# The first ten blocks of a mixer's input projection multiplied as whole fp32, without their split into two parts

## The chip, the cores and the metric

The kernel runs on one core of a Trainium2 chip. The metric is the device time of one execution in microseconds (us), the median of several runs. The engines are named PE (TensorE, matmuls), PEld (its weight loads), DVE (VectorE), ACT (ScalarE), POOL (GpSimd) and SP (SyncE, which here issues the loads from memory). Each runs its own list of instructions in order and waits on semaphores.

## What is computed

Two transformer blocks over 256 tokens of width 1024, all in fp32. The change sits in the first layer of the second block, in its mixer:

```python
h = x @ w_in
q, f_pre, i_v, g, a, a_gate = jnp.split(h, [...], axis=-1)   # six times 512 columns
f = lb + (1.0 - lb) * jax.nn.sigmoid(f_pre)                  # gated linear attention: f, k, q, v
k = (1.0 - lb) * jax.nn.sigmoid(-f_pre)
# heads: chunkwise scan over q, k, v, log f, then a norm and a gate with g
# convolution: u = a * sigmoid(a_gate), 31 taps over time per channel, layer norm, silu
# y = concat(heads, convolution) @ w_out
```

In front of it stands the end of the first block: `h + sigmoid(norm(h) @ w_ple_gate + b) * norm(p @ w_ple_proj)`, whose result is the mixer's x.

## The kernel before

All weights come as a stream of blocks of 128 x 1024 fp32 (512 KB), 8 tiles of 128 x 128 each. The list `LAYOUT` (L76) gives their order; around the change it is `ple_gate` (8 blocks), `ab_in` (20), `ab_g` (4), `mem1b` (4), `ab_out` (8). The ring of raw buffers `w_raw` has `RAW` = 4 places, the rings `w_hi` and `w_lo` of the parts `RING` = 4.

To get fp32 accuracy from the faster fp32r matmuls, each block is split: ACT writes `w_hi`, the rounded copy (`part_hi`, L499 to L506), and DVE writes the remainder `w_lo` = `w_raw` - `w_hi` (`part_lo`, L1012 to L1016). x is split likewise into `x_hi` and `x_lo`. `three` (L1803) issues three matmuls per tile: hi with hi, hi with lo, lo with hi (L1805 to L1807). `chunk` (L1813) does a block of 8 tiles this way with 256 moving columns and then counts up `block_done`.

Order is written out by hand. Each engine calls `blk()` once per block; on ACT and DVE that issues the parts of the block four further on (`behind`). So block b's parts are made while TensorE is at block b - 4. `w_hi` of block b waits for its load and for the end of block b - 4; SP loads block b when `lo_ready` says that the remainder of block b - 4 is made, since the raw buffer is free from then on (L472).

The 20 blocks of `ab_in` are, by n in the loops at L875 (ACT), L1646 (DVE) and L2338 (PE): n = 0 to 7 the pairs of convolution value and gate for the four channel groups, 8 to 11 f, 12 to 15 q, 16 to 19 the values. For odd n under 8, ACT takes the sigmoid of the gate (L879) and DVE forms the product into `ub` (L1652). The convolution runs on DVE: `conv_taps` (L1608) issues the next taps, 31 for each of 4 channel groups, 124 in all, each a multiply-add over 128 x 256 (L1620; the first of a group is L1617). `beside` (L1645) says how many stand behind each n, `comes` (L1605) from which total on a group may begin; of the two lowest open groups it alternates. A tap waits for the tap before it of its own group. Six more stand at L1672, up to eight around each head's state scan (L1688, L1691), and the rest behind (L1701).

x of the mixer is written by DVE (`embed`, L1579): the gate block c of `ple_gate` is scaled (L1589), ACT takes its sigmoid (L867), DVE multiplies (L1582) and adds into `xs` (L1583, `res_ready`). Then ACT makes `x_hi` (L871) and DVE `x_lo` (L1597), and TensorE's first two `ab_in` blocks go tile by tile together (`two_chunks`, L1822).

Behind the heads, ACT's list has the remaining `mem1b` blocks (L936), then `x_hi` of the heads (L947), then the norm of the convolution (L949). TensorE's output projection (L2437) starts when DVE has made `x_lo` of the heads (L1738).

Of the kernel before, what the change touches and what calls it, by code (L numbers as in the profile page):

```python
# [16 lines left out]
P = 128  # L17
# [25 lines left out]
TILES = 8  # L43
# [39 lines left out]
for _name, _count in LAYOUT:  # L83
    FIRST[_name] = NB
    NB += _count

# [58 lines left out]
def build(nc, x_d, mem_d, pT, prm_d, id_d, cst_d, late_d, w_d, out):  # L145
    with ExitStack() as ctx:
# [307 lines left out]
        def _(sp):  # L454
# [8 lines left out]
            for b in range(RAW, NB):  # L463
# [8 lines left out]
                sp.wait_ge(lo_ready, b - RAW + 1)  # L472
# [22 lines left out]
        def _(act):  # L495
# [3 lines left out]
            def part_hi(b):  # L499

                act.wait_ge(raw_in[b % RAW], 16 * (b // RAW + 1))
                if b >= RING:
                    act.wait_ge(block_done, b - RING + 1)
                if FIRST["pool"] <= b < FIRST["pool"] + 2:
                    act.wait_ge(pool_w, b - FIRST["pool"] + 1)
                nc.scalar.activation(w_hi[:, b % RING, :], w_raw[:, b % RAW, :], ACT.Copy).then_inc(hi_ready, 1)  # L506

            def behind(b):

                if b + RING < NB:  # L510
                    part_hi(b + RING)
# [424 lines left out]
            mem_blocks(1, 4, 6)  # L936
# [57 lines left out]
        def _(dve):  # L994
# [17 lines left out]
            def part_lo(b):  # L1012

                dve.wait_ge(hi_ready, b + 1)
                nc.vector.tensor_tensor(w_lo[:, b % RING, :], w_raw[:, b % RAW, :], w_hi[:, b % RING, :].bitcast(F32),  # L1015
                                        ALU.subtract).then_inc(lo_ready, 1)  # L1016

            def behind(b):

                if b + RING < NB:  # L1020
# [578 lines left out]
            embedded_lo(0, 2)  # L1599
            embed(DC - 1)  # L1600
            embedded_lo(2, DC)
# [3 lines left out]
            taps, made, comes = [0] * CC, [0] * CC, (0, 9, 20, 31)  # L1605
# [39 lines left out]
            beside = {1: 9, 3: 11, 5: 11, 7: 5, 8: 6, 9: 6, 10: 5, 11: 5, 12: 4, 13: 1, 14: 4, 15: 2, 16: 0, 17: 2, 18: 4, 19: 4}  # L1645
# [25 lines left out]

            conv_taps(6)  # L1672
# [120 lines left out]
        def _(pe):  # L1793
# [6 lines left out]
            def arrived(b):  # L1800
                pe.wait_ge(lo_ready, b + 1)
# [7 lines left out]
            def tile(b, n, w=P):  # L1809
                s = slice(n * P, n * P + w)  # L1810
                return w_hi[:, b % RING, s], w_lo[:, b % RING, s]
# [63 lines left out]
            def token_turns(blocks, outs, chunks, hi, lo, start, stop, first=None, ready=None, between=None, ahead=0):  # L1875

                for t in range(2):
                    s = slice(t * P, (t + 1) * P)
                    for i, b in enumerate(blocks):
                        if t == 0 and i >= ahead:  # L1880
                            arrived(b)
                        for k, c in enumerate(chunks[i]):
# [3 lines left out]
                            w = (ahead_hi[i][:, o], ahead_lo[i][:, o]) if i < ahead else (w_hi[:, b % RING, o], w_lo[:, b % RING, o])  # L1886
# [22 lines left out]
            def token_rows(b, outs, chunks, w, hi, lo, start, stop=False, ready=None):  # L1909

                arrived(b)
                for k, c in enumerate(chunks):
                    if ready:
                        ready(c)
                    for t in range(2):
                        s, o = slice(t * P, (t + 1) * P), slice(k * w, (k + 1) * w)
                        ins = three(outs[t][:, 0:w], hi[:, c, s], lo[:, c, s], w_hi[:, b % RING, o], w_lo[:, b % RING, o],
# [3 lines left out]
            def token_last(b, outs, chunks, hi, lo):  # L1921

                arrived(b)
                for t in range(2):
                    s = slice(t * P, (t + 1) * P)
                    for k, c in enumerate(chunks):
                        o = slice(k * HALF, (k + 1) * HALF)
                        ins = three(outs[t][:, :], hi[:, c, s], lo[:, c, s], w_hi[:, b % RING, o], w_lo[:, b % RING, o],
# [710 lines left out]
```

## Time and profile before

| | us |
|---|---|
| median of 3 runs | 1341.74 (1340.62 to 1345.08) |
| the profiled execution, its own time | 1341.19 |
| its span, first to last instruction | 1339.2 |
| PE busy | 1283.6 (96%) |
| DVE busy | 869.7 (65%) |
| ACT busy | 664.6 (50%) |

The rows below are of the profiled execution, with times counted from the start of its span. In a timeline a row can stand for several instructions of the same kind in a row (xN); its time is then from the start of the first to the end of the last. In brackets stand the idle time ahead of it and what ended it. Neighbouring matmuls overlap, so a matmul's cost in a queue is the distance between two starts and not its duration. The mixer's stage lies between about 592 and 752 us.

### The profile page before, as it was taken

Reading aid. Unit: us, or ns where it says so; the run is one execution under the profiler, and the core shown is the slowest. Engines: PE = TensorE matmul, PEld = TensorE weight load, DVE = VectorE, ACT = ScalarE, POOL = GpSimd, SP = SyncE. Lnnn points to the kernel's source line nnn. Section 1 sums busy time; section 2 is a strip of 40 time slices with the busy share of each in tenths; the row PEclk is TensorE's granted clock in tenths of the full one; section 3 lists DMA queues with packets and bytes.
Section 4 is the critical chain, followed back from the end, with each engine's and each line's share of the span. In section 5 each row is a group of like instructions: output and inputs, shape, how many; then the busy total and the mean of one; then the engine's idle time right before and its main releaser. Section 6 shows DMA issues by size and latency. Waiting matters only on the chain.

```text
span 1339.2 us, 18113 instructions
## 1 busy us (share of the span) xinstructions
PE 1283.6 (96%) x7204; PEld 1115.2 (83%) x7204; DVE 869.7 (65%) x1443; ACT 664.6 (50%) x995; POOL 5.3 (0%) x7
## 2 busy tenths in 40 slices
PE   8999999999999999999888899999999999999997
PEld 7888888997788888899877787788888987788886
DVE  5665567878676555679997665545557664654555
ACT  5654446657464444555614544544444554544443
POOL 0000000000000000000000000000001000000000
PEclk9999999999999999999978999999999999999999
DMA  7555555532455555454422432555554532455551
GB/s 280 175 188 190 187 186 187 189 115 80 147 176 185 188 188 186 149 174 158 158 79 95 143 126 95 205 175 186 189 179 151 174 127 95 157 174 181 189 185 58
DMA packets 61571, 215.84 MB, mean 161 GB/s; under 512 B 6576, under 2 KB 9904, under 8 KB 61232
## 3 DMA queue, kind: packets, MB, share of 16 engines
q1 hardware_dynamic: 61056, 213.15, 46.2%
q10 hardware_dynamic: 432, 1.54, 0.3%
q8 instruction: 57, 0.93, 0.3%
q14 instruction: 26, 0.21, 0.0%
HBM read 213.62 MB, written 1.05 MB: 160 GB/s over the span
## 4 chain that ended last, share of the span: by engine, by line
PE 80%; DVE 13%; ACT 4%; issue 1%; DMA 1%; SPq 0%; ACTq 0%; DVEq 0%
PE bank L1805 24%; PE bank L1807 24%; PE bank L1806 24%; DVE w_lo L1015 3%; DVE arena L1620 3%; PE bank L1985 1%; PE bank L1872 1%; ACT w_hi L506 1%; PE bank L2083 1%; PE bank L2123 1%; ACT xs L645 1%; DMA w_raw<-weights_d 1%; PE bank L2094 1%; DVE xs L1691 0%; DVE rt L1065 0%
## 5 line engine op out<-in xcount | busy, mean ns | idle before, releaser
L1015 DVE TENSOR_TENSOR w_lo<-w_raw,w_hi 128x1024 fp32r<-128x1024 f32 x395 | 481.9, 1225 | 368.4 <-ACT w_hi L506 367.2
L506 ACT ACTIVATE w_hi<-w_raw 128x1024 fp32r<-128x1024 f32 x395 | 416.7, 1059 | 537.7 <-PE bank L1807 525.6
L1805 PE MATMUL bank<-w_hi,x_hi 128*128 128x512 f32 (+2 forms) x992 | 372.7, 376 | 13.2 <-DVE x_lo L1033 6.6
L1807 PE MATMUL bank<-w_hi,x_lo 128*128 128x512 f32 (+2 forms) x992 | 367.2, 370 | 0.0
L1806 PE MATMUL bank<-w_lo,x_hi 128*128 128x512 f32 (+2 forms) x992 | 367.0, 370 | 0.0
L1805 PEld LDWEIGHTS bank<-w_hi,x_hi 128*128 128x128 f32 x992 | 187.1, 189 | 48.9 <-issue 10.9
L1807 PEld LDWEIGHTS bank<-w_hi,x_lo 128*128 128x128 f32 x992 | 186.9, 188 | 31.8
L1806 PEld LDWEIGHTS bank<-w_lo,x_hi 128*128 128x128 f32 x992 | 187.2, 189 | 30.2
L1805 PE MATMUL bank<-w_hi,h_hi 128*128 128x512 f32 (+1 forms) x364 | 142.3, 391 | 0.0
L1807 PE MATMUL bank<-w_hi,h_lo 128*128 128x512 f32 (+1 forms) x364 | 141.3, 388 | 0.0
L1806 PE MATMUL bank<-w_lo,h_hi 128*128 128x512 f32 (+1 forms) x364 | 141.2, 388 | 0.0
L1805 PE MATMUL bank<-x_hi,w_hi 128*128 128x256 f32 x352 | 102.7, 292 | 8.1 <-DVE x_lo L1033 2.9
L1806 PE MATMUL bank<-x_lo,w_hi 128*128 128x256 f32 x352 | 100.2, 285 | 0.0
L1807 PE MATMUL bank<-x_hi,w_lo 128*128 128x256 f32 x352 | 100.1, 284 | 0.0
L1805 PEld LDWEIGHTS bank<-w_hi,h_hi 128*128 128x128 f32 x364 | 68.4, 188 | 14.7 <-DVE h_lo L1033 1.2
L1807 PEld LDWEIGHTS bank<-w_hi,h_lo 128*128 128x128 f32 x364 | 68.3, 188 | 14.1
L1806 PEld LDWEIGHTS bank<-w_lo,h_hi 128*128 128x128 f32 x364 | 68.4, 188 | 13.4
L1805 PEld LDWEIGHTS bank<-x_hi,w_hi 128*128 128x128 f32 x352 | 68.1, 193 | 10.1 <-DVE w_lo L1015 3.8
L1806 PEld LDWEIGHTS bank<-x_lo,w_hi 128*128 128x128 f32 x352 | 68.1, 194 | 0.2
L1807 PEld LDWEIGHTS bank<-x_hi,w_lo 128*128 128x128 f32 x352 | 68.1, 193 | 0.0
L1620 DVE SCALAR_TENSOR_TENSOR arena<-arena,prm 128x256 f32<-128x256 f32 x120 | 50.8, 478 | 0.6
L1805 PE MATMUL bank<-m_hi,w_hi 128*128 128x256 f32 x128 | 38.7, 302 | 0.0
(307 smaller groups left out, 1390.4 us busy)
## 6 DMA issues: line engine op xcount, KB each, us to landing
w_raw<-weights_d SPq DMA_DIRECT2D x395, 512.0 KB, 3.2
arena<-weights_d SPq DMA_DIRECT2D x4, 512.0 KB, 6.2
arena<-late_d SPq DMA_DIRECT2D x1, 1056.0 KB, 5.7
xs<-x_d SPq DMA_DIRECT2D x2, 512.0 KB, 5.9
kv_mem<-mem_d ACTq DMA_DIRECT2D x1, 1024.0 KB, 7.2
out_d<-xs SPq DMA_DIRECT2D x4, 256.0 KB, 2.8
cst<-cst_d SPq DMA_DIRECT2D x1, 671.0 KB, 10.2
arena<-pT_d ACTq DMA_DIRECT2D x1, 256.0 KB, 2.7
```

What stands on the lines that cost most here:

```text
L506: nc.scalar.activation(w_hi[:, b % RING, :], w_raw[:, b % RAW, :], ACT.Copy).then_inc(hi_ready, 1)
L645: nc.scalar.activation(xs[:, c, 0, s], turned_n(v, c, t), ACT.Identity, scale=col("ln_g", LN_COL[v] + c), bias=col("ln_b", LN_COL[v] + c)) ...
L1015: nc.vector.tensor_tensor(w_lo[:, b % RING, :], w_raw[:, b % RAW, :], w_hi[:, b % RING, :].bitcast(F32), ALU.subtract).then_inc(lo_ready, 1)
L1620: ins = nc.vector.scalar_tensor_tensor(conv[:, c, :], src, w, conv[:, c, :], ALU.mult, ALU.add)
L1805: nc.tensor.matmul(out, wh, xh, start=start, stop=False, skip_group_check=True)
L1806: nc.tensor.matmul(out, wh, xl, start=False, stop=False, skip_group_check=True)
L1807: return nc.tensor.matmul(out, wl, xh, start=False, stop=stop, skip_group_check=True)
L1872: nc.tensor.matmul(PB[banks[t]][:, c % 4 * P:c % 4 * P + P], xs[:, c, 0, t * P:(t + 1) * P], res_i, start=False, stop=False, skip_group_ch ...
L1985: ins = nc.tensor.transpose(PB[2 + k][:, at:at + P], hf[:, t, (2 * k + j) * P:(2 * k + j + 1) * P], ident)
L2083: ins = nc.tensor.matmul(half(n % 2, t), xq[:, 2 * h + k, t * P:(t + 1) * P], k_mem[l][:, 2 * h + k, :], start=k == 0, stop=k == 1)
L2094: ins = nc.tensor.transpose(PB[2 + n % 2][:, k * S + t * P:k * S + (t + 1) * P], e_buf(n)[:, 0, t, k * P:(k + 1) * P], ident)
L2123: ins = nc.tensor.matmul(o[:, c * S:(c + 1) * S], v_mem[l][:, k, at:at + P], pt_buf(n)[:, k, :], start=k == 0, stop=k == 1)
```

## The change

The blocks n = 0 to 9 of `ab_in` (`WHOLE`) are no longer split. TensorE multiplies `w_raw` by `xs` in one fp32 matmul per tile (`whole_chunk`), as soon as the block's load has landed and the chunk of x is written. ACT and DVE leave out their parts. The parts are counted and placed by `parts_of` and `slot`, which leave the whole blocks out, instead of by the block's number. The raw buffer of a whole block is free when `block_done` says that TensorE has finished it, so SP waits for that. `two_chunks` is no longer used for `ab_in`; each block goes by itself.

The taps are dealt out anew: `beside` has 90 instead of 79 taps in the loop, `comes` is (0, 12, 26, 40), and the six taps behind the loop are gone (they stand in the rest at the end). On ACT one `mem1b` block is moved behind `x_hi` of the heads. On DVE the last `embed` comes ahead of all `x_lo`.

```diff
+WHOLE = range(FIRST["ab_in"], FIRST["ab_in"] + 10)
+def parts_of(b):
+    return b + 1 - min(max(b + 1 - WHOLE.start, 0), len(WHOLE))
+def slot(b):
+    return (parts_of(b) - 1) % RING
+def slot_before(b):
+    c = b - 1
+    while c >= 0 and (c in WHOLE or parts_of(c) != parts_of(b) - RING):
+        c -= 1
+    return c
...
-                sp.wait_ge(lo_ready, b - RAW + 1)
+                if b - RAW in WHOLE:
+                    sp.wait_ge(block_done, b - RAW + 1)
+                else:
+                    sp.wait_ge(lo_ready, parts_of(b - RAW))
                 sp.dma_start(w_raw[:, b % RAW, :], w_d[b]).then_inc(raw_in[b % RAW], 16)
...
-                if b >= RING:
-                    act.wait_ge(block_done, b - RING + 1)
+                if slot_before(b) >= 0:
+                    act.wait_ge(block_done, slot_before(b) + 1)
...
-                if b + RING < NB:
+                if b + RING < NB and b + RING not in WHOLE:
                     part_hi(b + RING)
...
-            mem_blocks(1, 4, 6)
+            mem_blocks(1, 4, 5)
...
             for h in range(HG_HEADS):
                 act.wait_ge(hy_f, h + 1)
                 nc.scalar.activation(x_hi[:, h, :], ho[:, h, :], ACT.Copy).then_inc(hy_hi, 1)
+            mem_blocks(1, 5, 6)
...
-                if b + RING < NB:
+                if b + RING < NB and b + RING not in WHOLE:
                     part_lo(b + RING)
...
-            embedded_lo(0, 2)
             embed(DC - 1)
-            embedded_lo(2, DC)
+            embedded_lo(0, DC)
...
-            taps, made, comes = [0] * CC, [0] * CC, (0, 9, 20, 31)
+            taps, made, comes = [0] * CC, [0] * CC, (0, 12, 26, 40)
...
-            beside = {1: 9, 3: 11, 5: 11, 7: 5, 8: 6, 9: 6, 10: 5, 11: 5, 12: 4, 13: 1, 14: 4, 15: 2, 16: 0, 17: 2, 18: 4, 19: 4}
+            beside = {1: 12, 3: 14, 5: 14, 7: 8, 8: 5, 9: 5, 10: 5, 11: 5, 12: 4, 13: 1, 14: 4, 15: 2, 16: 0, 17: 3, 18: 4, 19: 4}
...
-            conv_taps(6)
-
...
+            def whole_chunk(b, out, x, ready):
+
+                pe.wait_ge(raw_in[b % RAW], 16 * (b // RAW + 1))
+                for k in range(TILES):
+                    ready(k)
+                    ins = nc.tensor.matmul(out, w_raw[:, b % RAW, k * P:(k + 1) * P], x[:, k, 0, :], start=k == 0, stop=k == TILES - 1)
+                ins.then_inc(block_done, 1)
...
-                if n == 0:
-                    two_chunks(b, (half(4, 0), half(5, 0)), x_hi, x_lo, operand(4))
-                elif 1 < n < 16:
-                    chunk(b, half(4 + n % 4, 0), x_hi, x_lo)
+                elif n < 2:
+                    pe.wait_ge(gate_z, 7 + n)
+                if b in WHOLE:
+                    whole_chunk(b, half(4 + n % 4, 0), xs, lambda k: pe.wait_ge(res_ready, k + 1))
+                elif n < 16:
+                    chunk(b, half(4 + n % 4, 0), x_hi, x_lo, operand(4))
```

## Rows read from the trace of the kernel before

**Rows 1.** The page, busy us and share of the span of each engine.
```profile
PE 1283.6 (96%) x7204; PEld 1115.2 (83%) x7204; DVE 869.7 (65%) x1443; ACT 664.6 (50%) x995; POOL 5.3 (0%) x7
```

**Rows 2.** The chain of waits from 560 to 760, its shares by line.
```profile
by line: DVE arena L1620 20.7%; DVE w_lo L1015 15.5%; PE bank L1805 11.3%; PE bank L1806 10.7%; PE bank L1807 10.7%; issue 3.4%; DVE xs L1691 3.2%; ACT w_hi L506 2.6%; PE bank L1872 1.8%; PE bank L2404 1.4%; PE bank L1865 1.3%; DVE arena L1
```

**Rows 3.** Busy time by stretch (length; PE, PEld, DVE, ACT, POOL; clock; DMA).
```profile
599.50:670.50 71.00, 63.96 (x532) 62.51 (x531) 67.94 (x120) 41.62 (x60) 0.00 (x0) 1.00 0.44 149
670.50:706.00 35.50, 27.15 (x209) 26.00 (x209) 32.57 (x78) 6.62 (x14) 0.00 (x0) 0.77 0.22 75
```

**Rows 4.** TensorE's timeline, 591 to 722 (start, us, instruction, idle before and releaser).
```profile
591.90 0.28 PE L1806 MATMUL bank<-x_lo,w_hi 128*128 128x256 f32 x1
592.02 0.28 PE L1807 MATMUL bank<-x_hi,w_lo 128*128 128x256 f32 x1
595.19 0.36 PE L1805 MATMUL bank<-x_hi,w_hi 128*128 128x256 f32 x1 [2.89 <-DVE x_lo L1033]
...
619.06 0.39 PE L1805 MATMUL bank<-x_hi,w_hi 128*128 128x256 f32 x1 [0.61 <-DVE arena L1652]
...
626.02 0.39 PE L1805 MATMUL bank<-x_hi,w_hi 128*128 128x256 f32 x1 [0.95 <-DVE arena L1652]
...
674.21 1.01 PE L2400 MATMUL bank<-arena 128*128 128x128 f32 x3 [6.81 <-DVE xs L1691]
...
705.99 0.69 PE L2416 MATMUL bank<-ident,arena 128*128 128x128 f32 x2 [3.40 <-DVE arena L1620]
...
721.33 0.47 PE L1805 MATMUL bank<-w_hi,x_hi 128*128 128x512 f32 x1 [1.90 <-DVE x_lo L1033]
```

**Rows 5.** TensorE's timeline near 792: whole fp32 matmuls, two records each.
```profile
792.23 1.89 PE L2123 MATMUL bank<-arena,kv_mem 128*128 128x256 f32 x8
793.96 1.89 PE L2083 MATMUL bank<-kv_mem,arena 128*128 128x256 f32 x8
```

**Rows 6.** DVE's timeline, 593 to 706.
```profile
593.12 0.42 DVE L1583 TENSOR_TENSOR xs<-bank,arena 128x256 f32<-128x256 f32 x1
...
602.07 2.36 DVE L1015 TENSOR_TENSOR w_lo<-w_raw,w_hi 128x1024 fp32r<-128x1024 f32 x2 [2.50 <-ACT w_hi L506]
...
605.26 4.13 DVE L1620 SCALAR_TENSOR_TENSOR arena<-arena,prm 128x256 f32<-128x256 f32 x8
...
618.92 4.43 DVE L1620 SCALAR_TENSOR_TENSOR arena<-arena,prm 128x256 f32<-128x256 f32 x11
...
625.55 0.42 DVE L1652 TENSOR_TENSOR arena<-bank,arena 128x256 f32<-128x256 f32 x1
...
634.88 1.21 DVE L1015 TENSOR_TENSOR w_lo<-w_raw,w_hi 128x1024 fp32r<-128x1024 f32 x1
...
670.43 1.22 DVE L1015 TENSOR_TENSOR w_lo<-w_raw,w_hi 128x1024 fp32r<-128x1024 f32 x1
...
685.09 1.23 DVE L1015 TENSOR_TENSOR w_lo<-w_raw,w_hi 128x1024 fp32r<-128x1024 f32 x1 [1.32 <-ACT w_hi L506]
...
700.49 5.43 DVE L1620 SCALAR_TENSOR_TENSOR arena<-arena,prm 128x256 f32<-128x256 f32 x11
```

**Rows 7.** ACT's timeline, 593 to 721.
```profile
593.36 0.49 ACT L867 ACTIVATE arena<-arena,prm 128x256 f32<-128x256 f32 x1
...
632.14 1.06 ACT L506 ACTIVATE w_hi<-w_raw 128x1024 fp32r<-128x1024 f32 x1 [0.18 <-PE bank L1807]
...
718.65 1.06 ACT L506 ACTIVATE w_hi<-w_raw 128x1024 fp32r<-128x1024 f32 x1 [1.99 <-PE bank L1807]
...
719.88 1.32 ACT L947 ACTIVATE x_hi<-arena 128x256 fp32r<-128x256 f32 x4
```

**Rows 8.** The weight loads of L473, all 391, from issue to landing.
```profile
DMA to landing us min/median/max: 3.0/3.2/7.3
```

**Rows 9.** Busy time in two stretches of 1 us, columns as in rows 3.
```profile
672.00:673.00 1.00, 0.00 (x0) 0.00 (x0) 0.93 (x3) 0.00 (x0) 0.00 (x0) 0.69 0.38 86
682.00:683.00 1.00, 1.00 (x8) 1.00 (x7) 1.00 (x4) 0.00 (x0) 0.00 (x0) 0.69 0.00 0
```

More of the change, by code:

```diff
@@ L1012, in part_lo @@
             def part_lo(b):
-                dve.wait_ge(hi_ready, b + 1)
-                nc.vector.tensor_tensor(w_lo[:, b % RING, :], w_raw[:, b % RAW, :], w_hi[:, b % RING, :].bitcast(F32),
+                dve.wait_ge(hi_ready, parts_of(b))
+                nc.vector.tensor_tensor(w_lo[:, slot(b), :], w_raw[:, b % RAW, :], w_hi[:, slot(b), :].bitcast(F32),
                                         ALU.subtract).then_inc(lo_ready, 1)
             def behind(b):
-                if b + RING < NB:
+                if b + RING < NB and b + RING not in WHOLE:
                     part_lo(b + RING)
@@ L1800, in arrived @@
             def arrived(b):
-                pe.wait_ge(lo_ready, b + 1)
+                pe.wait_ge(lo_ready, parts_of(b))
             def three(out, wh, wl, xh, xl, start=False, stop=False):
@@ L1810, in tile @@
                 s = slice(n * P, n * P + w)
-                return w_hi[:, b % RING, s], w_lo[:, b % RING, s]
+                return w_hi[:, slot(b), s], w_lo[:, slot(b), s]
             def chunk(b, out, hi, lo, ready=None):
@@ L1885, in token_turns @@
                             o = slice(k * HALF, (k + 1) * HALF)
-                            w = (ahead_hi[i][:, o], ahead_lo[i][:, o]) if i < ahead else (w_hi[:, b % RING, o], w_lo[:, b % RING, o])
+                            w = (ahead_hi[i][:, o], ahead_lo[i][:, o]) if i < ahead else (w_hi[:, slot(b), o], w_lo[:, slot(b), o])
                             ins = three(outs[t][:, :], hi[:, c, s], lo[:, c, s], *w,
@@ L1916, in token_rows @@
                         s, o = slice(t * P, (t + 1) * P), slice(k * w, (k + 1) * w)
-                        ins = three(outs[t][:, 0:w], hi[:, c, s], lo[:, c, s], w_hi[:, b % RING, o], w_lo[:, b % RING, o],
+                        ins = three(outs[t][:, 0:w], hi[:, c, s], lo[:, c, s], w_hi[:, slot(b), o], w_lo[:, slot(b), o],
                                     start=start and k == 0, stop=stop and k == len(chunks) - 1)
@@ L1927, in token_last @@
                         o = slice(k * HALF, (k + 1) * HALF)
-                        ins = three(outs[t][:, :], hi[:, c, s], lo[:, c, s], w_hi[:, b % RING, o], w_lo[:, b % RING, o],
+                        ins = three(outs[t][:, :], hi[:, c, s], lo[:, c, s], w_hi[:, slot(b), o], w_lo[:, slot(b), o],
                                     stop=k == len(chunks) - 1)
@@ L2208, in _ @@
                     s = slice(t * P, (t + 1) * P)
-                    ins = three(PB[first + t][:, :], h_hi[:, 2, s], h_lo[:, 2, s], w_hi[:, b % RING, part:part + 512],
-                                w_lo[:, b % RING, part:part + 512], start=True, stop=True)
+                    ins = three(PB[first + t][:, :], h_hi[:, 2, s], h_lo[:, 2, s], w_hi[:, slot(b), part:part + 512],
+                                w_lo[:, slot(b), part:part + 512], start=True, stop=True)
                 ins.then_inc(signal, 1)
@@ L2247, in _ @@
                         o = slice(4 * QK * g, 4 * QK * (g + 1))
-                        ins = three(PB[2 * t + g][:, 0:4 * QK], h_hi[:, k, s], h_lo[:, k, s], w_hi[:, b % RING, o], w_lo[:, b % RING, o],
+                        ins = three(PB[2 * t + g][:, 0:4 * QK], h_hi[:, k, s], h_lo[:, k, s], w_hi[:, slot(b), o], w_lo[:, slot(b), o],
                                     start=k == 0, stop=k == 1)
@@ L2472, in _ @@
                         ins = three(PB[Z_BANK[8][g // 2][t]][:, g % 2 * S:g % 2 * S + S], x_hi[:, 2 * g + k, s], x_lo[:, 2 * g + k, s],
-                                    w_hi[:, b % RING, o], w_lo[:, b % RING, o], start=g % 2 == 0 and k == 0)
+                                    w_hi[:, slot(b), o], w_lo[:, slot(b), o], start=g % 2 == 0 and k == 0)
                     if t and g % 2:
```

2 lines of the change are left out of this document (1 added, 1 removed).

## The prediction

> **What bounds the kernel now.** First the page's busy shares: TensorE (PE) is busy 96% of the span [rows 1], so most of the kernel ends when TensorE ends. The change sits in one stage, the mixer of the second block, so next comes the chain of waits cut to 560:760. There the dearest lines are not matmuls but VectorE's (DVE's): taps (L1620) 20.7% and weight remainders w_lo (L1015) 15.5%, against some 11% for each of the three matmul lines [rows 2]. Third, the busy table by stretch: from 599.5 to 670.5 DVE is busy 67.94 of 71 us, from 670.5 to 706 it is busy 32.57 of 35.5, while TensorE has slack in the second [rows 3]. Fourth, TensorE's timeline, for where it stops [rows 4]: 2.89 us at 595.19 (for x_lo), 0.61 and 0.95 at 619.06 and 626.02 (for the gate product L1652), 6.81 at 674.21 (for the state scan), 3.40 at 705.99 (for the last tap), 1.90 at 721.33 (for x_lo of the heads). So what counts from 600 to 706 is when DVE finishes its in-order list; ahead of that and behind it TensorE's own list counts.
>
> **Part 1, whole blocks on TensorE.** A tile now costs three fp32r matmuls at one per 0.12 us (591.90 to 592.02) [rows 4], 0.36 us; a block of 8 tiles takes 2.88. A whole tile is one fp32 matmul of the same 128x128 by 256. The trace has them in fours, each as two records: x8 from 792.23 to the next group's start at 793.96 is 1.73 us for four, 0.4325 each [rows 5]. Eight make 3.46 us, ten blocks 34.6 against 28.8: 5.8 us more of TensorE. I take 0.4325: same shape, same engine, full clock. Upper bound: if no record overlapped the next, each would take the last record's 1.89 - 7 x 0.216 = 0.38, or 0.76 per tile [rows 5].
>
> The rows price the whole tile at 1.2 times the three matmuls. The Trainium skill, "FP8 and Floating Point Precision", section TensorE Precision Notes, says that true FP32 takes four passes through the array. At the split's row pitch that would be 4 x 0.12 = 0.48 a tile and 9.6 us more instead of 5.8; the rows show less, and the measurement decides for the forecast.
>
> **Part 2, the start of the stage.** Before, TensorE's last record of the gate blocks starts at 592.02 and the next only at 595.19, since x_hi and x_lo come first [rows 4]. A whole block waits for xs instead. With no w_hi ahead of it in ACT's queue the last sigmoid (L867, at 593.36 now) starts near 592.9; DVE's last sum but one is written at 593.12 + 0.42, and the last, without the 1.23 us w_lo behind it, at about 594.4 [rows 6, 7]. TensorE reads tile 6 at 592.14 + 6 x 0.4325 = 594.7 and tile 7 at 595.2, so block 0 starts at 592.14 and doesn't stop. That returns 2.9 us plus the two gate waits (1.6), nearly all of the 5.8: block 10 (the first split one) starts at 592.14 + 34.6 = 626.7, against 626.02 [rows 4].
>
> **Part 3, DVE's list up to block 10.** Ten w_lo leave DVE (four before 594, six between 602 and 624), some 1.14 us of queue each, and ten w_hi leave ACT. x_hi and x_lo stay, for blocks 10 on; they run beside blocks 0 and 1 now, whose 6.9 us hide them (without this cover they would cost the 2.9 us of part 2 again). The new numbering of ring places changes only indices. Taps cost 0.52 when one channel group follows itself (x8 in 4.13) and 0.40 when two alternate (x11 in 4.43) [rows 6]. Gate product c needs TensorE's block 2c+1, then a sigmoid, then 0.42 us [rows 6]: some 1.2 us behind the block's end.
> - Product 0 ends at 599.1 + 1.2 = 600.3; 12 taps alone, 6.2, to 606.5.
> - Product 1 (block 3 ends at 606.0) ends at 607.2; 14 taps, 5.6, to 612.8.
> - Product 2 (block 5 ends at 612.9) ends at 614.1; 14 taps to 619.7.
> - Now a new wait. The raw buffer of a whole block is free only when TensorE has finished it. Block 10's load starts when block 6 ends, 616.4 + 0.3, and lands 3.2 later (median; 3.0 to 7.3) [rows 8] at 619.9; w_hi 1.06 and w_lo 1.14 put its remainder at 622.2, where DVE would have been free at 619.7. Block 11 (freed at 619.8) gives 625.6. Behind that waiting w_lo stand, on DVE, product 3 and all taps; TensorE waits for product 3 at block 10 (626.0 against 626.7: 0.7 us to spare). ACT's sigmoid of block 7 queues behind the same w_hi. SP issues loads in order, so loads 14 and on stand behind load 13, which waits for block 9 (626.7); w_lo 14 is due at 635.5, which covers it.
> - 8 taps to 629.2; w_lo 12, 5 taps, w_lo 13, 5 taps, to 635.5.
>
> At the same point before, DVE stands at 634.88 [rows 6]. So it is 0.6 us later, but has issued 58 taps instead of 48. ACT is 3 to 4 us later in blocks 10 to 12 (w_hi 15 at 636.6 against 632.14 [rows 7]), which takes up slack that it has again before the scan.
>
> **Part 4, the rest of the taps.** From there to the end of the loop n, 37 taps become 32 (L1672's 6 go, n=17 gets one more): 5 x 0.40 = 2.0 less. w_lo at 670.43 [rows 6] comes at 669.0, 1.4 earlier; so does the state scan, and TensorE's 6.8 us stop at 674.21 shrinks by it. The heads' 28 taps stay. Of the last 11 taps (700.49, 5.43 us) [rows 6] 6 remain, at 0.52 since only group 3 is left: 3.1; but five of the taps ahead of them now follow their own group, 5 x 0.12 = 0.6. Gain 5.4 - 3.1 - 0.6 = 1.7. The last tap ends 3.1 us earlier.
>
> **Part 5, ACT's order behind the heads.** Before, x_hi of the heads (719.88) stands behind a w_hi that waits for TensorE (718.65) [rows 7]. Moved ahead of it, x_hi can start some 3 us earlier (an estimate from the order of the two queues), and TensorE's 1.90 us stop at 721.33 [rows 4] goes; the gated conv norm moves earlier too and is not next. 1.8 taken, 0 to 1.9 possible.
>
> **Sum.** -3.1 - 1.8 = -4.9 us. After 721 TensorE runs its own list and passes it on. The profiled execution took 1341.19 (span 1339.2 and 2.0 around it), 0.55 under the median of the runs: 1336.3 by it, 1336.8 for the median.
>
> **Rivals.**
> - *Same, the whole tile or the load is dearer.* At 0.48 a tile, block 7 ends 3.0 us later, and with it DVE's release at w_lo 11: 3 us of gain gone, 1339.8. A landing of 6 us instead of 3.2 does the same. For: landings of up to 7.3 exist [rows 8]. Against: the four-matmul rows, and a queue with hardly a second load in flight.
> - *Slower, whole tiles don't overlap.* With every tile waiting for its own two weight loads and results, pitch rises towards 0.76: 80 x 0.33 = 26 us more on TensorE, of which the stage's waits hide none, since DVE already waits for each product; 1358. It turns slower by 4 us from a pitch of (4.0 + 4.9) / 80 + 0.43 = 0.54. Against: [rows 5] show them overlapping in fours; but no row has a run of eighty.
> - *More gain, clock.* The granted clock is 0.69 in 672:673 and again 0.69 in 682:683, the lower of the two levels (1.2 GHz) between, after the idle 667 to 674 [rows 9]; the mean of 670.5 to 706 is 0.77 [rows 3]. DVE's wait of 1.32 us at 685.09, for a w_hi behind a slow block [rows 6], is its price on the path. If the shorter idle (5 us instead of 7) keeps 2.4 GHz, that goes too: 1335.5. If instead the low level lasts longer, the two blocks behind 706 cost up to 2.2 us each more, and the result falls into the first rival.
>
> **How the numbers follow.** Forecast, 1335.9 to 1338.3: 0.48. More gain: 0.17. Dearer tile or load, 1338.3 to 1341.5: 0.25. Slower: 0.10. A measurement can tell about 0.3%, 4.0 us: faster means under 1337.7. That is the second case and three quarters of the first, 0.53; the rest of the first and nearly all of the third are the same, 0.36; slower 0.11. The range, 1334.0 to 1341.5, takes in the bounds of the load and the tile at 0.48 and leaves out the case of no overlap.
>
> **What would show it.** Right: no TensorE gap at the stage's start; whole matmuls of 2 records at 0.216 us; first split block near 626.7; DVE idle in front of w_lo 10 and 11 by 1.4 and 2.2 us with a w_hi, and behind it a load, as releaser; last tap near 702.8; TensorE not stopping for x_lo before the output projection. Wrong: a pitch over 0.45, TensorE stopping at block 10 for product 3, or the low clock lasting longer between 667 and 715.

## The result, and the profile of the changed kernel

The changed kernel takes 1337.18 us (median of 5 runs, 1335.99 to 1337.96), against 1341.74 for the kernel before: a ratio of 0.9957, 95% interval 0.9939 to 0.9975. It is faster by 4.6 us, 0.43%, against the 0.3% that the prediction set as the least that can be told; the upper end of the interval, 0.9975, falls just short of that bound. The forecast was 1336.8, within 1334.0 to 1341.5. The profiled execution took 1337.18 with a span of 1335.4; that of before 1341.19 and 1339.2.

The page of the changed kernel, busy us of each engine, answers to [rows 1]:

```profile
PE 1290.4 (97%) x7124; PEld 1118.3 (84%) x7124; DVE 858.8 (64%) x1433; ACT 654.3 (49%) x985; POOL 5.3 (0%) x7
```

TensorE has exactly 80 matmul records fewer (80 tiles of two records in place of three) and yet 6.8 us more work. DVE has ten instructions and 10.9 us less, ACT ten and 10.3 us less. The busiest engine has more to do and the kernel is shorter, so the page alone can't explain it. The busy table by stretch does. Its columns are length; PE, PEld, DVE, ACT, POOL; clock; DMA share and GB/s. The first two lines answer to [rows 3]:

```profile
599.50:670.50 71.00, 66.63 (x456) 62.26 (x454) 64.58 (x118) 35.21 (x54) 0.00 (x0) 1.00 0.51 169
670.50:706.00 35.50, 30.07 (x220) 28.86 (x221) 32.06 (x82) 6.62 (x14) 0.00 (x0) 0.76 0.23 78
706.00:721.40 15.40, 15.40 (x109) 14.90 (x108) 13.32 (x42) 10.48 (x22) 0.00 (x0) 0.88 0.24 77
```

In the first stretch TensorE took on 2.7 us and DVE lost 3.4. That is the trade: work that DVE did in the way of its list went to an engine that was waiting.

TensorE's timeline of the changed kernel, where it stops or changes its kind of work (start, us, instruction, idle before and releaser). It answers to [rows 4]; the lines are about 20 further down in the code (L1805 is now L1825, L1620 is L1642), and L1847 is the whole-tile matmul:

```profile
592.72 0.81 PE L1847 MATMUL bank<-xs,w_raw 128*128 128x256 f32 x3
...
627.07 0.47 PE L1825 MATMUL bank<-x_hi,w_hi 128*128 128x256 f32 x1
...
673.26 1.22 PE L2430 MATMUL bank<-arena 128*128 128x128 f32 x4 [4.91 <-DVE xs L1711]
...
703.45 0.69 PE L2446 MATMUL bank<-ident,arena 128*128 128x128 f32 x2 [1.43 <-DVE arena L1642]
703.79 0.56 PE L1825 MATMUL bank<-m_hi,w_hi 128*128 128x256 f32 x1
704.15 0.41 PE L1826 MATMUL bank<-m_lo,w_hi 128*128 128x256 f32 x1
704.36 0.41 PE L1827 MATMUL bank<-m_hi,w_lo 128*128 128x256 f32 x1
...
717.59 0.48 PE L1825 MATMUL bank<-w_hi,x_hi 128*128 128x512 f32 x1
```

The 2.89 us stop at the stage's start and the two stops for the gate product are gone; the stop for the state scan fell from 6.81 to 4.91, that for the last tap from 3.40 to 1.43, and the output projection at 717.59 starts without the 1.90 us stop.

DVE's timeline, same columns, answers to [rows 6]:

```profile
600.31 0.42 DVE L1674 TENSOR_TENSOR arena<-bank,arena 128x256 f32<-128x256 f32 x1 [1.33 <-ACT arena L901]
...
621.37 1.23 DVE L1038 TENSOR_TENSOR w_lo<-w_raw,w_hi 128x1024 fp32r<-128x1024 f32 x1 [1.35 <-ACT w_hi L528]
624.98 1.22 DVE L1038 TENSOR_TENSOR w_lo<-w_raw,w_hi 128x1024 fp32r<-128x1024 f32 x1 [2.38 <-ACT w_hi L528]
...
684.40 1.23 DVE L1038 TENSOR_TENSOR w_lo<-w_raw,w_hi 128x1024 fp32r<-128x1024 f32 x1 [1.58 <-ACT w_hi L528]
...
700.31 3.08 DVE L1642 SCALAR_TENSOR_TENSOR arena<-arena,prm 128x256 f32<-128x256 f32 x6
703.31 1.42 DVE L1726 TENSOR_TENSOR arena<-arena 128x256 f32<-128x256 f32 x4
```

And ACT's, with the transfer as the releaser of the two w_hi that DVE waits for:

```profile
620.28 1.06 ACT L528 ACTIVATE w_hi<-w_raw 128x1024 fp32r<-128x1024 f32 x1 [6.26 <-DMA w_raw<-weights_d]
623.88 1.06 ACT L528 ACTIVATE w_hi<-w_raw 128x1024 fp32r<-128x1024 f32 x1 [2.55 <-DMA w_raw<-weights_d]
```

**One measure for all kernels.** The kernels reach this stage between 591.5 and 592.7 us, before anything that the change touches in it. So times below are counted from the place of the first whole tile (for kernels without whole blocks: 0.12 us behind the last record of the gate blocks) to the start of the output projection's first matmul. For before that is 592.14 to 721.33, 129.2 us; for the changed kernel 592.72 to 717.59, 124.9. The difference, 4.3, is nearly all of the 4.6 us between the medians. Behind the projection these two run alike: 721.33 and 717.59 differ by 3.7 (the changed kernel reached the stage 0.6 us later), the spans by 3.8. From the projection to the end it is 617.9 us in the one and 617.8 in the other.

### The profile page after: what moved, and what is told of

The parts are those of the page before. It is cut to its first block, busy times and chain, and to the rows that moved or that the text cites. A ratio compares the mean times of both kernels' runs of the same rounds, so it can differ in the third digit from the quotient of the medians.

```text
span 1335.4 us, 17924 instructions
## 1 busy us (share of the span) xinstructions
PE 1290.4 (97%) x7124; PEld 1118.3 (84%) x7124; DVE 858.8 (64%) x1433; ACT 654.3 (49%) x985; POOL 5.3 (0%) x7
## 4 chain that ended last, share of the span: by engine, by line
PE 82%; DVE 11%; ACT 4%; issue 1%; DMA 1%; SPq 0%; DVEq 0%; ACTq 0%
PE bank L1825 24%; PE bank L1827 24%; PE bank L1826 24%; DVE w_lo L1038 3%; PE bank L1847 2%; DVE arena L1642 2%; PE bank L2013 1%; PE bank L1900 1%; ACT w_hi L528 1%; PE bank L2111 1%; PE bank L2151 1%; DMA w_raw<-weights_d 1%; ACT xs L667 1%; PE bank L2122 1%; DVE xs L1711 0%
## 5 line engine op out<-in xcount | busy, mean ns | idle before, releaser
L1038 DVE TENSOR_TENSOR w_lo<-w_raw,w_hi 128x1024 fp32r<-128x1024 f32 x385 | 469.9, 1225 | 370.1 <-ACT w_hi L528 368.7
L528 ACT ACTIVATE w_hi<-w_raw 128x1024 fp32r<-128x1024 f32 x385 | 406.0, 1059 | 525.2 <-PE bank L1827 500.2
L1825 PE MATMUL bank<-w_hi,x_hi 128*128 128x512 f32 (+2 forms) x992 | 372.7, 376 | 11.9 <-DVE w_lo L1038 5.2
L1825 PEld LDWEIGHTS bank<-w_hi,x_hi 128*128 128x128 f32 x992 | 187.1, 189 | 47.2 <-issue 9.3
L1825 PE MATMUL bank<-w_hi,h_hi 128*128 128x512 f32 (+1 forms) x364 | 142.3, 391 | 0.0
L1825 PE MATMUL bank<-x_hi,w_hi 128*128 128x256 f32 x272 | 80.1, 295 | 3.7 <-ACT kv_mem L697 1.7
L1825 PEld LDWEIGHTS bank<-w_hi,h_hi 128*128 128x128 f32 x364 | 68.4, 188 | 14.7 <-DVE h_lo L1056 1.2
L1826 PE MATMUL bank<-x_lo,w_hi 128*128 128x256 f32 x272 | 77.7, 286 | 0.0
L1827 PE MATMUL bank<-x_hi,w_lo 128*128 128x256 f32 x272 | 77.6, 285 | 0.0
L1825 PEld LDWEIGHTS bank<-x_hi,w_hi 128*128 128x128 f32 x272 | 52.9, 194 | 5.1 <-ACT kv_mem L697 1.9
L1826 PEld LDWEIGHTS bank<-x_lo,w_hi 128*128 128x128 f32 x272 | 52.9, 195 | 0.2
L1827 PEld LDWEIGHTS bank<-x_hi,w_lo 128*128 128x128 f32 x272 | 52.9, 194 | 0.0
L1642 DVE SCALAR_TENSOR_TENSOR arena<-arena,prm 128x256 f32<-128x256 f32 x120 | 51.2, 477 | 0.7
L1825 PE MATMUL bank<-m_hi,w_hi 128*128 128x256 f32 x128 | 39.2, 306 | 0.0
```

The source lines that it names most:

```text
L528: nc.scalar.activation(w_hi[:, slot(b), :], w_raw[:, b % RAW, :], ACT.Copy).then_inc(hi_ready, 1)
L1038: nc.vector.tensor_tensor(w_lo[:, slot(b), :], w_raw[:, b % RAW, :], w_hi[:, slot(b), :].bitcast(F32), ALU.subtract).then_inc(lo_ready, 1)
L1642: ins = nc.vector.scalar_tensor_tensor(conv[:, c, :], src, w, conv[:, c, :], ALU.mult, ALU.add)
L1825: nc.tensor.matmul(out, wh, xh, start=start, stop=False, skip_group_check=True)
L1826: nc.tensor.matmul(out, wh, xl, start=False, stop=False, skip_group_check=True)
L1827: return nc.tensor.matmul(out, wl, xh, start=False, stop=stop, skip_group_check=True)
```

## The experiments

The theory: TensorE's extra work lies under DVE's list; the time is that of the last tap, and five parts set it: the taps' new deal, the ten w_lo gone, two waits for a raw buffer, the low clock level behind the scan, and ACT's order behind the heads. The experiments take four of them one by one; the ten w_lo are tried only together with the rest. Two things were not run: the new deal of the taps in the kernel before, where DVE is busy 67.94 of 71 us already [rows 3], and the new place of the last `embed` on DVE. Kernels are compared with runs of the kernel before made beside them: 1342.48 for ACT's order put back, the old deal of taps and the two kernels with five buffers; 1342.91 for the changed kernel again, ACT's order alone, the nine taps and the fourteen products; 1341.90 for the last two. The last tap's end is read as the start of DVE's next instruction.

### ACT's order put back in the changed kernel

```diff
-            mem_blocks(1, 4, 5)
+            mem_blocks(1, 4, 6)
...
                 nc.scalar.activation(x_hi[:, h, :], ho[:, h, :], ACT.Copy).then_inc(hy_hi, 1)
-            mem_blocks(1, 5, 6)
```

> The changed kernel with one part undone: on ACT both mem1b blocks stand again ahead of x_hi of the heads. My sum gave this part 1.8 us. If that is right, TensorE stops again for x_lo before the output projection by about 2 us, and the time is about 1339.2 (ratio to the kernel before 0.998). Rival: another wait (the ho norm, w_lo of the first projection block) stands right behind, and the order is worth nothing: 1337.2.

Measured: 1337.50 (1336.38 to 1338.49), ratio 0.9965 [0.9953, 0.9978]. The stop is back, in TensorE's timeline of this kernel:

```profile
717.73 0.47 PE L1824 MATMUL bank<-w_hi,x_hi 128*128 128x512 f32 x1 [1.91 <-DVE x_lo L1055]
```

The last tap ends 110.6 us after the first whole tile, as in the changed kernel (592.72 to 703.31), and from there to the projection it takes 15.6 us instead of 14.3. So the order is worth 1.3 us between these two traces; they differ in the clock too, and Part 5 below compares at like clock. The median went up by only 0.3 to 0.5, less than the runs can tell; the 1339.2 did not come, so these runs alone settle neither the term's size nor that it is nothing.

### ACT's order alone, in the kernel before

```diff
-            mem_blocks(1, 4, 6)
+            mem_blocks(1, 4, 5)
...
                 nc.scalar.activation(x_hi[:, h, :], ho[:, h, :], ACT.Copy).then_inc(hy_hi, 1)
+            mem_blocks(1, 5, 6)
```

> The kernel before with only the new order on ACT (x_hi of the heads ahead of the last mem1b block). TensorE's stop of 1.90 us at 721.33 should go, and x_lo of the heads should come 2 us earlier: 1.8 us gained, ratio 0.9987. Undoing this part in the changed kernel moved the time by only 0.3 us although the stop came back with 1.91 us. Rival from that: the stop goes, but TensorE is held by something else (slower clock, next block's w_lo) and the ratio is 0.9995 to 1.000.

Measured: 1342.03 (1340.51 to 1342.77, 11 runs), ratio 0.9993 [0.9984, 1.0001]. In the trace the stop at the projection is gone and the last tap's end is 13.6 us ahead of it (708.90 to 722.50) instead of 15.5 (705.85 to 721.33): 1.9 us. Its last tap came 3.2 us later than before, and most of that was lost at the start of the stage, where the clock of this execution stood low and that of before did not:

```profile
595.05 0.56 PE L1806 MATMUL bank<-x_hi,w_hi 128*128 128x256 f32 x1 [2.90 <-DVE x_lo L1034]
595.40 0.41 PE L1807 MATMUL bank<-x_lo,w_hi 128*128 128x256 f32 x1
```

The granted clock is 0.51 from 594 to 601, and the first gate product on DVE starts at 606.81 instead of 604.35, 2.6 us later on the stage's own clock; the low stretch behind the scan is also 3.4 us longer (672.7 to 686.3, against 672.4 to 682.6 before). The median moved by 0.9, within its interval. The mean granted clock of these 11 runs is 0.984, that of the runs of before beside them 0.985; whether the order brings the longer low stretches or chance does is open. So the mechanism is shown: a stop of 1.9 us that the order removes. How much of it reaches the total isn't settled by either median.

### The whole blocks with the old deal of the taps

```diff
-            taps, made, comes = [0] * CC, [0] * CC, (0, 12, 26, 40)
+            taps, made, comes = [0] * CC, [0] * CC, (0, 9, 20, 31)
...
-            beside = {1: 12, 3: 14, 5: 14, 7: 8, ...}
+            beside = {1: 9, 3: 11, 5: 11, 7: 5, ...}
...
+            conv_taps(6)
```

> The changed kernel with the old deal of the taps (79 in the loop, 6 behind it, groups beginning at 0, 9, 20, 31), all else as changed. By my sum DVE is held until about 625.6 by the loads of blocks 10 and 11 whatever it has done before, so ten taps more lie behind that point: 4 us less 0.4 that n=8 and n=9 hold, and the last tap ends about 3.3 us later; time about 1340.5, ratio 0.999. The whole blocks alone are then worth about 1 us plus what the ACT order brings. Rival: DVE does the same taps in the end, only at other places, and the freed w_lo are what counts: 1337.2 to 1338.

Measured: 1340.05 (11 runs, 1338.37 to 1342.64), ratio 0.9982 [0.9973, 0.9991]. DVE's timeline shows where the freed time went when no taps were put into it:

```profile
606.84 0.42 DVE L1674 TENSOR_TENSOR arena<-bank,arena 128x256 f32<-128x256 f32 x1 [1.80 <-ACT arena L901]
613.74 0.42 DVE L1674 TENSOR_TENSOR arena<-bank,arena 128x256 f32<-128x256 f32 x1 [2.08 <-ACT arena L901]
621.24 1.23 DVE L1038 TENSOR_TENSOR w_lo<-w_raw,w_hi 128x1024 fp32r<-128x1024 f32 x1 [2.72 <-ACT w_hi L528]
```

The waits of the changed kernel at the same three places are 0.24, 0.89 and 1.35. The last tap comes later, as the theory has it (3.3 forecast, 3.6 measured). The stop for the state scan is 6.80 us, as before the change (6.81), that for the last tap 3.40 again, and the last tap ends 114.2 us after the first whole tile, 3.6 later than in the changed kernel. Before, it ended 113.7 us after that place, so up to the last tap the whole blocks alone gain nothing (0.5 lost): w_lo removed from a list that then waits for TensorE's products saves nothing by itself. What is left of the gain here, 2.4 us of medians, has its place behind the last tap, where this kernel has ACT's new order: 13.3 us to the projection (706.56 to 719.86) instead of 15.5.

### Five raw weight buffers in the changed kernel

```diff
-RAW = 4
+RAW = 5
```

> The changed kernel with five raw buffers instead of four, so that the loads of blocks 10 and 11 can be issued one block (3.46 us) earlier. If DVE's 3.7 us of waits in front of w_lo 10 and 11 are caused by the late release of the raw buffers, both vanish, and the stage ends about 3.5 us earlier: 1333.8, ratio 0.994. Rival: DVE reaches the later points earlier only to wait there for ACT (logf, sigmoids) or TensorE, and the time stays at 1337.2.

Measured: 1333.84 (1333.23 to 1335.02), ratio 0.9939 [0.9926, 0.9951]. The wait at w_lo 10 is gone and that at w_lo 11 fell from 2.38 to 0.38:

```profile
619.04 1.21 DVE L1038 TENSOR_TENSOR w_lo<-w_raw,w_hi 128x1024 fp32r<-128x1024 f32 x1
620.63 1.22 DVE L1038 TENSOR_TENSOR w_lo<-w_raw,w_hi 128x1024 fp32r<-128x1024 f32 x1 [0.38 <-ACT w_hi L528]
```

The last tap ends 107.2 us after the first whole tile instead of 110.6, the stage is 120.8 us long. The change had put a new wait on the path, and it cost 3.4 us of its gain.

### Five raw weight buffers in the kernel before

The same edit in the kernel before, as the control: is it the wait for whole blocks, or would more buffers help anyway?

> Control: the kernel before with five raw buffers. There the raw buffer is freed by w_lo, well ahead of the need, and the fifth buffer should change nothing in the mixer: 1341.7, ratio 1.000 within 0.001. If loads elsewhere in the kernel are late, it is faster, and the same share of the run with five buffers on the changed kernel isn't the mixer's.

Measured: 1342.46 (11 runs, 1340.85 to 1345.94), ratio 1.000 [0.999, 1.001]; the stage is 129.3 us long, against 129.2. In these two kernels the fifth buffer is worth something only where a buffer must wait for TensorE.

### The changed kernel again

> The changed kernel itself, as the measure for the three runs beside it: 1337.2, ratio 0.9957.

Measured: 1336.96 (1336.46 to 1337.93), ratio 0.9958 [0.9945, 0.9971]; DVE's two waits are 1.43 and 2.21 us, the last tap ends 111.0 us after the first whole tile, the stage is 124.5. From the last tap to the projection it is 13.5 us here, 0.8 less than in the first execution.

### Nine more taps ahead of DVE's two waits

```diff
-            taps, made, comes = [0] * CC, [0] * CC, (0, 12, 26, 40)
+            taps, made, comes = [0] * CC, [0] * CC, (0, 12, 26, 49)
...
-            beside = {1: 12, 3: 14, 5: 14, 7: 8, ... 12: 4, 13: 1, 14: 4, ...}
+            beside = {1: 12, 3: 14, 5: 17, 6: 6, 7: 8, ... 12: 2, 13: 1, 14: 2, ...}
```

> The changed kernel with nine more taps in front of DVE's two waits (17 at n=5, 6 at n=6, group 3 from tap 49 on; two fewer each at n=12 and n=14, five fewer at the end). If DVE's 3.7 us of waits for w_hi 10 and 11 are idle time on the path, as five raw buffers said, nine taps of 0.40 us fit into them and the last tap ends 3.3 us earlier or more: 1333.9, ratio 0.9935. Rival: the gain with five buffers came from earlier loads elsewhere, and filling the wait brings under 1 us: 1336.5.

Measured: 1335.02 (1330.72 to 1337.07), ratio 0.9943 [0.9929, 0.9957]. DVE's timeline:

```profile
620.37 1.22 DVE L1038 TENSOR_TENSOR w_lo<-w_raw,w_hi 128x1024 fp32r<-128x1024 f32 x1 [0.32 <-ACT w_hi L528]
...
682.99 1.23 DVE L1038 TENSOR_TENSOR w_lo<-w_raw,w_hi 128x1024 fp32r<-128x1024 f32 x1 [2.12 <-ACT w_hi L528]
...
699.80 1.42 DVE L1726 TENSOR_TENSOR arena<-arena 128x256 f32<-128x256 f32 x4
701.99 0.17 DVE L1729 TENSOR_SCALAR rv<-bank 128x8 f32<-128x8 f32 x1 [0.76 <-PE bank L2440]
```

The waits for w_hi went from 1.35 and 2.38 to 0.32 and nothing, and the last tap came 108.2 us after the first whole tile, 2.4 to 2.8 earlier. But now it is TensorE that is late behind it: DVE waits 0.76 us for its row sums, and from the last tap to the projection it takes 15.8 us. In this trace 1.5 to 2.3 us of what DVE won were lost again behind the last tap, where TensorE ran at the low level from 698.6 to 705.4 and was busy all of 699 to 705.5. The median says more than the trace (2 us below the changed kernel), but the runs spread over 6 us: that DVE's waits can be filled with taps is shown, the 1333.9 neither met nor refuted.

### TensorE kept busy with products of nothing new

This kernel adds fourteen fp32 products of hq by the identity, into a bank that is overwritten before it is read; it leaves nothing out.

```diff
-                pe.wait_ge(st_ready, h + 1)
                 if h >= 2:
                     pe.wait_ge(ho_sq, h - 1)
+                for _ in range((9, 0, 2, 0)[h]):
+                    nc.tensor.matmul(PB[4][:, 0:S], ident, hq[:, 0, :], start=True, stop=True)
+                pe.wait_ge(st_ready, h + 1)
...
             for c in range(CC):
+                if c == CC - 1:
+                    for _ in range(3):
+                        nc.tensor.matmul(PB[4][:, 0:S], ident, hq[:, 0, :], start=True, stop=True)
                 pe.wait_ge(conv_done, c + 1)
```

> The changed kernel plus 14 whole fp32 matmuls whose result nobody reads, put into TensorE's idle times in front of the state scans of heads 0 and 2 (9 and 2) and in front of the last tap (3). They cost TensorE 6.1 us that it would have waited anyway. If the granted clock falls because of these idle times, it stays at 2.4 GHz through the heads and behind the last tap; DVE's wait of 1.58 us for a w_hi near 684 goes, and from the last tap to the output projection it takes 12.9 instead of 14.2 us: about 3 us gained, 1334.2, ratio 0.994. Rival: the clock has other causes or isn't on the path: 1337.2, or slower where the added matmuls hold up a state scan.

Measured: 1335.41 (1332.91 to 1336.01), ratio 0.9942 [0.9930, 0.9954]. The busy table of this kernel in two stretches, and TensorE's timeline at the last tap (L2448 are the added products here):

```profile
667.00:697.00 30.00, 25.64 (x219) 23.50 (x217) 29.01 (x70) 7.95 (x16) 0.00 (x0) 1.00 0.25 88
697.50:704.00 6.50, 6.50 (x27) 5.85 (x27) 5.93 (x23) 0.25 (x1) 0.00 (x0) 0.50 0.24 83
```

```profile
698.34 1.52 PE L2451 MATMUL bank<-ident,arena 128*128 128x128 f32 x6
699.65 2.77 PE L2448 MATMUL bank<-arena,ident 128*128 128x256 f32 x6
702.21 0.63 PE L2451 MATMUL bank<-ident,arena 128*128 128x128 f32 x2
```

With the idle ahead of the first head filled, the clock holds 2.4 GHz through 667 to 697, where the changed kernel stands at 0.50 twice (672.0 to 682.3 and 692.5 to 695.9). It isn't this execution alone: the mean granted clock is 0.990 to 0.994 over the five runs of this kernel and 0.985 to 0.988 over the ten of the changed one. The last tap, at 700.00, ends 108.4 us after the first whole tile, 2.6 less than in the changed kernel beside it. The three products ahead of the last transposes did harm: the clock had been low since 697.5, before the first of them started at 699.65, so each took 0.85 us, and TensorE was at the transposes 2.2 us behind the last tap. They came too late to show whether work there would have kept the clock up. The clock's price ahead of the last tap is shown, and that this form of it pays in full isn't: 1334.2 was expected. From the projection to the end this trace takes 619.0 us, the two of the changed kernel 617.8 and 618.0, so about 1.1 us of the gain went again there: the next low stretch is 6.8 us long (745.3 to 752.1), the changed kernel's 3.4 (750.5 to 753.9).

### The same without the three products at the last tap

```diff
-                if c == CC - 1:
-                    for _ in range(3):
-                        nc.tensor.matmul(PB[4][:, 0:S], ident, hq[:, 0, :], start=True, stop=True)
```

> The changed kernel with eleven added fp32 products of nothing new (TensorE multiplies hq by the identity into a bank that is overwritten before it is read; nine while it waits for head 0's statistics, two before head 2's), and none ahead of the last transposes, where three of them stood in TensorE's way in the kernel before this one. Theory A (the last tap sets the time; the head products bring it 2.6 us earlier, and the three tail products cost 2.2 us between the last tap and the transposes): last tap 2.6 us earlier against the first whole product than in the changed kernel, 1336.96 - 2.6 = 1334.4, and below the kernel with the tail products. Theory B (the clock's fall is only put off: what the head products keep at full clock is paid back behind the last tap whether or not tail products stand there): the way from the last tap to the output projection is 14.6 us or more in place of 13.5, and the time is 1335.4 or more.

Measured: 1334.57 (1333.97 to 1336.58, 4 runs), ratio 0.9941 [0.9924, 0.9958]. The last tap ends 108.6 us after the first whole tile, 2.4 less than in the second run of the changed kernel, and 13.1 us lie between it and the projection. The median is that of theory A (1334.4), though the intervals of this kernel and of the changed one overlap, and theory B's 1335.4 lies inside this kernel's interval. TensorE's timeline and the busy table of this kernel:

```profile
701.00 0.69 PE L2448 MATMUL bank<-ident,arena 128*128 128x128 f32 x2 [1.36 <-DVE arena L1642]
```

```profile
683.00:687.00 4.00, 4.00 (x30) 3.88 (x25) 3.82 (x12) 0.38 (x2) 0.00 (x0) 0.57 0.40 135
```

TensorE is at the last transposes 0.14 us behind the last tap, in place of 2.2. That is the cost of the three products; the ratios, 0.9942 and 0.9941, don't show it. The 14.6 and 13.1 us compare it only roughly, for here the last low stretch is 3.4 us long (700.5 to 703.9) and with the fourteen products it is 6.8 (697.5 to 704.3). The kernel in the next section, with eleven products and a last low stretch of 6.8 us, takes 13.3. So the 14.6 us or more of theory B came in neither trace.

Two things here limit what the added work does. The clock fell all the same, from 683.4 to 686.8, with the idle filled and TensorE busy. And from the projection to the end this trace takes 620.8 us, 3.0 more than the changed kernel: the next low stretch is 6.8 us long here too (from 744.8), and another of 3.4 comes at 792.6, where the changed kernel has none; 1.2 and 1.7 us are lost about these two. That is all that the stage had gained: the spans are 1334.8 here and 1335.4 and 1334.7 in the two traces of the changed kernel. This execution is the slowest of the four, and the median is 2.4 us below the changed kernel's. Theory B in a wider form, that full clock in the heads is in part paid back later in the kernel, is therefore not ruled out. Against it stands the kernel with nine taps moved, which adds no work to TensorE and takes 619.1 us from the projection to the end as well.

### Five buffers and the eleven products together

The kernel before this one with `RAW = 5`.

> The changed kernel with a fifth raw weight buffer and the same eleven added head products. The two gains lie at different places on VectorE's way to the last tap (3.1 us of waiting for raw blocks 10 and 11; about 2.6 us of TensorE work at the low clock level behind it). If they add: 1333.8 - 2.6 = 1331.2. If the five-buffer gain only shifts the stretches of low clock as it did alone (its last tap came 3.8 us earlier against the first whole product, 107.2 in place of 111.0) and the added products then miss the idle time that they are meant to fill: 1333 to 1334, no better than five buffers alone.

Measured: 1330.87 (1330.04 to 1331.74, 4 runs), ratio 0.9915 [0.9900, 0.9930]. The stretches, TensorE's stop for the state scan and DVE's last tap in this kernel:

```profile
664.00:692.00 28.00, 24.18 (x206) 22.04 (x205) 27.01 (x67) 7.29 (x14) 0.00 (x0) 1.00 0.28 96
694.50:700.00 5.50, 5.50 (x26) 5.12 (x27) 5.02 (x20) 0.00 (x0) 0.00 (x0) 0.50 0.27 92
```

```profile
668.55 0.71 PE L2432 MATMUL bank<-arena 128*128 128x128 f32 x4 [0.45 <-DVE xs L1711]
```

```profile
696.35 1.43 DVE L1726 TENSOR_TENSOR arena<-arena 128x256 f32<-128x256 f32 x4
```

The last tap ends 104.9 us after the first whole tile, and the stage is 118.2 us long. The two gains add within what the runs can tell: against before 11.0 us, where five buffers gave 8.6 and the eleven products on top were to give 2.6 more. This kernel is faster than both the kernel before and the changed one; its interval and that of five buffers alone overlap a little (0.9930 and 0.9926). All stages side by side, in us:

| kernel | first whole tile to last tap | to the projection | median, less that of before beside it |
|---|---|---|---|
| before | 113.7 | 129.2 | 0 |
| changed | 110.6 | 124.9 | -4.6 |
| changed, again | 111.0 | 124.5 | -6.0 |
| ACT's order back | 110.6 | 126.2 | -5.0 |
| ACT's order alone | 116.9 | 130.5 | -0.9 |
| old deal of taps | 114.2 | 127.5 | -2.4 |
| five raw buffers | 107.2 | 120.8 | -8.6 |
| five, in before | 113.8 | 129.3 | 0.0 |
| nine taps moved | 108.2 | 124.0 | -7.9 |
| fourteen products | 108.4 | 122.9 | -7.5 |
| eleven products | 108.6 | 121.7 | -7.3 |
| five and eleven | 104.9 | 118.2 | -11.0 |

The stage is one execution, the median many; where they differ by 2 to 3 us, neither is taken as exact. What follows the stage is not the same in all: from the projection to the end it takes 617.8 to 618.2 us in the first six kernels of the table, 618.5 to 618.9 with five buffers, and 619.0 to 620.8 with nine taps moved and the fourteen or eleven products on four buffers.

## Why the prediction was right, step by step

**Part 1, the whole tile.** Ten blocks took 592.72 to 627.07, 34.35 us or 0.4294 a tile, against 34.6 and 0.4325. The four-matmul rows [rows 5] were the right price, and a run of eighty overlaps as well as one of four. The rivals of a dearer tile and of tiles that don't overlap are out.

The 0.48 that followed from four passes at the split's pitch (the Trainium skill, "FP8 and Floating Point Precision", TensorE Precision Notes) is not what came. With the gap that "TensorE: Matmul & The Clock Gate" of the Trainium skill gives in its section "Wait — 56ns, not 53.3ns?" (N / 2.4 GHz + 2.5 ns), four passes of 256 make an estimate of 0.437 if the gap is counted for each pass, and 0.429 if it is counted once for the whole matmul. The trace's 0.4294 agrees with the second.

**Part 2, the start.** Right: no stop, 2.89 and the two gate waits returned, and the first split block started at 627.07, 626.5 on the clock of the kernel before, against 626.7.

**Part 3, DVE's list.** On the stage's own clock (0.6 subtracted) the three products ended at 600.1, 607.0 and 613.9, against 600.3, 607.2 and 614.1. The new waits were 1.35 and 2.38 us, against 1.4 and 2.2 as the difference of the steps, with w_hi as the releaser and the transfer behind it. The five-buffer kernels show that this chain was real and what it cost. TensorE did not stop for product 3 at block 10. w_lo 14 came at 635.2, against 635.5.

**Part 4, the taps.** The last tap ended at 703.31 - 0.6 = 702.7, against 705.85: 3.1 us earlier, as forecast. The stop for the scan shrank by 1.9, against 1.4. The last six taps took 3.08, against 3.1.

**Part 5, ACT's order.** The mechanism was right, the stop went, but in this execution the term was mis-sized: 1.8 was taken, and from last tap to projection the trace shows 15.5 before and 14.3 after, 1.2 us. The missing part lies in the clock. The low level ended at nearly the same time in both (709.9 and 709.6), but the changed kernel's last tap and the work behind it lie 2.5 us earlier and so deeper in it. At 704.15 and 704.36 the split matmuls start 0.21 us apart, against 0.12 at full clock. The busy table of the kernel before and of the changed one over that stretch:

```profile
703.50:709.50 6.00, 3.52 (x17) 3.52 (x18) 5.48 (x21) 0.00 (x0) 0.00 (x0) 0.50 0.00 0
```

```profile
703.00:709.50 6.50, 6.05 (x29) 6.05 (x30) 6.02 (x26) 1.28 (x4) 0.00 (x0) 0.50 0.02 6
```

TensorE did 2.5 us more of its work there, at half the clock; at full clock that would have been some 1.2 us. The prediction had named a longer low level as the downside, but not this form of it: the stretch stays where it is and the work moves into it. How long the low level lasts behind the last tap (read from the granted clock, in us) tells the traces apart:

| kernel | low level behind the last tap | last tap to the projection |
|---|---|---|
| *with the stop for x_lo* | | |
| before | 4.1 | 15.5 |
| five, in before | 4.1 | 15.5 |
| ACT's order back | 4.3 | 15.6 |
| *with ACT's new order* | | |
| eleven products | 3.0 | 13.1 |
| five and eleven | 4.0 | 13.3 |
| old deal of taps | 4.0 | 13.3 |
| changed, again | 4.5 | 13.5 |
| five raw buffers | 4.7 | 13.6 |
| ACT's order alone | 4.7 | 13.6 |
| changed | 6.2 | 14.3 |

Where the low level reaches 4.0 to 4.7 us behind the last tap, in both groups, the order is worth 2.0 to 2.2 us, a little more than the 1.8 taken and the 1.9 given as the most. In the profiled execution of the changed kernel the low level took some 0.8 us of it back. The two kernels in which TensorE is late for another reason, nine taps moved and fourteen products, are left out. This is a comparison of traces; the medians don't show it as clearly (next paragraph).

**The sum.** In the two traces of the changed kernel -3.1 - 1.2 = -4.3 and -2.7 - 2.0 = -4.7, against -4.9; in the medians -4.6 and -6.0. The median of the kernel with ACT's order put back is only 0.3 to 0.5 us above that of the changed one, so how the medians divide between the two terms stays open. That the total came within 0.4 us of the forecast in the first set of runs is in part luck: the second set gave 6.0.

**The clock rival.** The shorter idle ahead of the scan (4.91 instead of 6.81) did not keep 2.4 GHz: the mean clock of 670.5 to 706 is 0.76 against 0.77 [rows 3]. DVE's wait near 685 stayed, 1.58 against 1.32. Filling that idle with work kept the level through the heads in two traces, and in the third the clock fell for 3.4 us in place of 13.7 or 17.1. On four buffers it returned 2.0 to 2.6 us up to the last tap, more than the 1.3 that the rival had put on it; over the whole kernel the medians gave 1.3 to 2.4 against the second set of runs of the changed kernel.

## What to carry to other kernels

Work taken off an engine with an in-order list is worth only what is put in its place: the same ten w_lo brought the last tap no earlier with the old deal of taps, and 2.7 to 3.1 us earlier with the new. When the consumer of a buffer changes, follow its release through the next load to the engines behind it: the waits of 1.4 and 2.4 us could be worked out from the profile's load time, they were on the path, and one more buffer removed all but 0.4 us of them. A low clock level costs twice, where DVE waits behind it and where work that comes earlier moves into it, so read such a stretch by its level and its place, not by its mean, and look behind the stage for what the next low stretches take back.

## What the runs showed of the hardware that was not expected

- A whole fp32 product of 128x128 by 256 costs 0.429 us in a run of eighty at 2.4 GHz and 0.85 at 1.2 GHz (six records from 699.65 to 702.21), against 0.36 for the three fp32r matmuls of the split.
- The clock fell to 1.2 GHz with TensorE busy: in the kernel with five buffers and eleven products TensorE is busy 3.00 of 3.00 us from 690.5 to 693.5 at 2.4 GHz, and at 693.5 the clock falls, to stay low until 700.3 (5.50 of 5.50 us busy in 694.50 to 700.00). The last idle ahead of it was 1.45 us, up to 690.49. The changed kernel has such a fall too, at 692.5, 2.4 us behind an idle of 1.24. What exactly brings these falls is open.
- The same program lies differently to the clock in different executions: in the changed kernel the last low stretch ran from 702.7 to 709.6 in one and from 700.9 to 707.7 in the other, and the one before it lasted 3.4 us in the one and 6.8 in the other. The kernel with only ACT's order changed had a low stretch at the start of the stage (594.1 to 601.0) that no other trace has, and it cost 2.6 us. So a single stage moves by 1 to 3 us, which is as much as most of the edits here are worth.
